# The last two chunks of the second down projection, its norm and the index queries by halves of the tokens

## The reference

```python
x = x + g2 * conv_ffn(h, ffn_w_up[i], ffn_conv_w[i], ffn_conv_b[i], ffn_w_down[i])   # end of layer 0
...
h = rms_norm(x, norm_mix[i]) * (1.0 + sc1) + sh1                                      # start of layer 1
...
proj = h @ w_in
q, lat, qi, ki, wi = jnp.split(proj, [o1, o2, o3, o4], axis=-1)
```

## Time and profile before

| | |
|---|---|
| median of 3 runs | 1906.05 us (1905.83 to 1906.07) |
| the profiled execution's own time | 1905.76 us |
| its span | 1904.0 us |
| busy: PE, PEld | 1877.8 us, 1529.4 us |
| busy: DVE, ACT, POOL | 1081.6 us, 522.3 us, 1189.4 us |

### The profile page before, as it was taken

One profiled execution on the slowest core, in us unless ns is written; L12 is line 12 of the kernel. 1 busy time (PEld: TensorE's weight loads), 2 busy tenths in 40 slices (PEclk: granted clock), 3 DMA queues, 4 the chain that ended last, 5 costly groups with the idle time before them and its releaser, 6 DMA issues.

```text
span 1904.0 us, 26991 instructions
## 1 busy us (share of the span) xinstructions
PE 1877.8 (99%) x9462; PEld 1529.4 (80%) x9462; DVE 1081.6 (57%) x1690; ACT 522.3 (27%) x1085; POOL 1189.4 (62%) x684
## 2 busy tenths in 40 slices
PE   9999899999999999999999999999999999999999
PEld 7867778888888877779888888877766798888887
DVE  5966589998786515654533442144988463433322
ACT  4135300000115424442212121133357331112110
POOL 7641798887665564345766666655757357666673
PEclk9999999999999999999999999989999999999999
DMA  7530277776552231115333333312211123233331
GB/s 280 194 108 3 88 262 240 258 253 220 195 172 78 86 111 56 56 46 176 99 99 99 93 94 99 98 62 85 89 34 34 45 67 116 94 99 99 90 97 66
DMA packets 62325, 221.03 MB, mean 116 GB/s; under 512 B 6907, under 2 KB 7163, under 8 KB 62124
## 3 DMA queue, kind: packets, MB, share of 16 engines
q1 hardware_dynamic: 45216, 161.58, 26.9%
q10 hardware_dynamic: 17036, 58.46, 8.5%
HBM read 217.87 MB, written 2.14 MB: 116 GB/s over the span
## 4 chain that ended last, share of the span: by engine, by line
PE 93%; DVE 3%; POOL 2%; issue 1%; ACT 1%; DMA 0%; SPq 0%; DVEq 0%; POOLq 0%; ACTq 0%
PE bank L332 25%; PE bank L334 25%; PE bank L333 25%; PE bank L974 2%; PE bank L995 1%; PE bank L986 1%; PE bank L367 1%; PE bank L368 1%; PE bank L1102 1%; PE bank L372 1%; PE bank L1154 1%; PE bank L1145 1%; PE bank L463 1%; PE bank L467 1%; PE bank L464 1%
## 5 line engine op out<-in xcount | busy, mean ns | idle before, releaser
L1616 POOL TENSOR_TENSOR w_lo<-raw,w_hi 128x1024 fp32r<-128x1024 f32 x298 | 762.4, 2558 | 24.8
L332 PE MATMUL bank<-a_hi,w_hi 128*128 128x512 f32 (+1 forms) x2000 | 760.3, 380 | 2.1 <-DVE tmp L2417 1.5
L334 PE MATMUL bank<-a_hi,w_lo 128*128 128x512 f32 (+1 forms) x2000 | 758.7, 379 | 0.0
L333 PE MATMUL bank<-a_lo,w_hi 128*128 128x512 f32 (+1 forms) x2000 | 758.6, 379 | 0.0
L1614 POOL TENSOR_SCALAR w_hi<-raw 128x1024 fp32r<-128x1024 f32 x298 | 341.7, 1147 | 597.4 <-PE bank L334 451.6
L332 PEld LDWEIGHTS bank<-a_hi,w_hi 128*128 128x128 f32 x2000 | 376.7, 188 | 74.0 <-DVE tmp L2417 2.0
L333 PEld LDWEIGHTS bank<-a_lo,w_hi 128*128 128x128 f32 x2000 | 376.7, 188 | 70.3
L334 PEld LDWEIGHTS bank<-a_hi,w_lo 128*128 128x128 f32 x2000 | 376.5, 188 | 70.5
L2161 DVE CUSTOM_DVE_ANT_0 y<-y,cond 128x1024 f32<-128x1024 f32 x84 | 209.9, 2532 | 0.0
L2176 DVE SCALAR_TENSOR_TENSOR tmp<-bank,vecs,tmp 128x511 f32<-128x511 f32 x88 | 65.9, 749 | 240.9 <-ACT tmp L1884 240.8
L1884 ACT ACTIVATE tmp<-bank,vecs 128x512 f32<-128x512 f32 x88 | 68.1, 779 | 351.1 <-PE bank L334 347.2
(11 more groups left out here) (314 smaller groups left out, 2113.2 us busy)
## 6 DMA issues: line engine op xcount, KB each, us to landing
raw<-in_stream SPq DMA_DIRECT2D x299, 512.0 KB, 3.5
y<-in_ada ACTq DMA_DIRECT2D x96, 512.0 KB, 4.6
x<-in_x SPq DMA_DIRECT2D x4, 512.0 KB, 6.8
bias<-in_bias ACTq DMA_DIRECT2D x1, 2048.0 KB, 13.5
y<-rel_rows ACTq DMA_DIRECT2D x1, 2048.0 KB, 8.2
bias<-rel_rows ACTq DMA_DIRECT2D x1, 2048.0 KB, 13.2
out<-x SPq DMA_DIRECT2D x8, 256.0 KB, 2.0
cond<-in_c ACTq DMA_DIRECT2D x1, 512.0 KB, 6.9
```

Of the source, the lines that this page charges most:

```text
L332: pe.matmul(o, lhs_hi, rhs_hi, start=start, stop=False, **kw)
L333: pe.matmul(o, lhs_hi, rhs_lo, start=False, stop=False, **kw)
L334: return pe.matmul(o, lhs_lo, rhs_hi, start=False, stop=stop, **kw)
L1616: pool.tensor_tensor(w_lo[:, s, :], raw[:, j, :], f32(w_hi[:, s, :]), ALU.subtract).then_inc(split_ready, 1)
```

## The change

The last two chunks of the second down projection are computed by halves of the tokens, in all eight banks: first half 0 of all tiles, then half 1, both in the order 5, 7, 4, 6, 0, 1, 2, 3. VectorE updates x by half tiles as they come (16 pieces; bank c is read in half 0 before TensorE goes on in its half 1). The norm "mix1" is made in two halves like the others, but with its running sum of squares in `square_sum`, since no bank is free. Its sums of half 0 are put behind the fourth tile of half 1, its spread behind the seventh. The qi tiles run by `pe_early_halves`. POOL makes no low parts of this norm any more; VectorE makes all of them. The first steps of `dve_halved_norm` that scale, take lows and take the inverse are moved to `dve_half_steps` unchanged. The numbering of semaphore counts is changed to fit and left out here.

```diff
-POOL_LOWS = {"battn": (1, 3, 5), "mix1": (1, 3, 5, 7)}
+POOL_LOWS = {"battn": (1, 3, 5)}
...
-HALVED = ("mix0", "ffn0", "ffn1")
+HALVED = ("mix0", "ffn0", "mix1", "ffn1")
...
+DOWN_ORDER = (5, 7, 4, 6, 0, 1, 2, 3)
+DOWN_PIECES = 2 * DC
...
+        def pe_down_halves(pe, name, last, norm):
+            for h in range(2):
+                for n, c in enumerate(DOWN_ORDER):
+                    if h:
+                        pe.wait_ge(x_ready, X_AT[name] + n + 1)
+                    for i in last:
+                        s, j = (START[name] + i) % SPLIT, i % 4
+                        m = pe_three_passes(pe, bank[c][:, tokens_of(h)], w_hi[:, s, c * P:(c + 1) * P], w_lo[:, s, c * P:(c + 1) * P],
+                                            a_hi[:, j, tokens_of(h)], a_lo[:, j, tokens_of(h)], False, i == FC - 1, skip_group_check=True)
+                        if h and n == DC - 1:
+                            m.then_inc(block_done, 1)
...
+                    if h and n == 3:
+                        pe.wait_ge(x_ready, X_AT[name] + DC + 1)
+                        pe_sum_half(pe, norm, 0)
+                    if h and n == 6:
+                        pe_spread_half(pe, norm, 0)
...
+        def act_down_norm(a, update, name, shift):
+            _, high = act_halves(a, update, name, shift)
+
+            def square(p):
+                c, cols = down_piece(p)
+                a.wait_ge(x_ready, X_AT[update] + p + 1)
+                if p % DC == 0:
+                    a.wait_ge(group_used, GROUP_AT[name] - 1)
+                    dst = square_sum[:, GROUP_AT[name] % 2, cols]
+                else:
+                    a.wait_ge(sq_added, down_added(name, p) - 1)
+                    dst = squares[:, down_added(name, p) % 2, cols]
+                a.activation(dst, x[:, c, cols], ACT.Square).then_inc(sq_ready, 1)
+
+            a.preload_act_table(ACT.Sqrt)
+            for p in range(DC + 2):
+                square(p)
+            act_rms(a, name, 0, half_columns(0))
+            for p in range(DC + 2, DC + 5):
+                square(p)
+            for c in range(3):
+                high(0, c)
+                square(DC + 5 + c)
+            for c in range(3, DC):
+                high(0, c)
...
-            pool_lows("mix1")
...
-            pe_down(pe, "down2", 1, norm="mix1")
-
-            pe_norm(pe, "mix1", 1)
-            pe_tiles(pe, "qi", "mix1")
+            pe_down(pe, "down2", 1, halved="mix1")
+            pe_early_halves(pe, "qi", "mix1", "down2", (DC + 6, DOWN_PIECES))
...
+        def dve_down_norm(v, update, name, layer, which, gain, shift):
+            group = square_sum[:, GROUP_AT[name] % 2, :]
...
+            def add(p):
+                added, cols = down_added(name, p), down_piece(p)[1]
+                v.wait_ge(sq_ready, SQUARE_AT[name] + p + 1)
+                v.wait_ge(sq_added, added)
+                v.tensor_tensor(group[:, cols], group[:, cols], squares[:, added % 2, cols], ALU.add).then_inc(sq_added, 1)
+
+            inverse, scale, low = dve_half_steps(v, name, gain, shift)
+            for p in range(DC):
+                residual(p)
+                if p > 1:
+                    add(p - 1)
+            residual(DC)
+            add(DC - 1)
+            residual(DC + 1)
+            residual(DC + 2)
+            inverse(0)
+            residual(DC + 3)
+            add(DC + 1)
+            add(DC + 2)
+            v.wait_ge(rstd_ready, NORM_INDEX[name] + 1)
+            for c in range(DC):
+                scale(0, c)
+                if c < 4:
+                    residual(DC + 4 + c)
+                if c:
+                    low(0, c - 1)
+                if 0 < c < 6:
+                    add(DC + 2 + c)
```

More of the change, by code:

```diff
@@ L601, in sum_columns @@
                 return rstd_bank[:, HALF:HALF + TT]
-            return (bank[0] if name in ("post_ffn", "mix1") else bank[4])[:, 0:TT]
+            return (bank[0] if name == "post_ffn" else bank[4])[:, 0:TT]
         def pe_sum_group(pe, name, g):
@@ L630, in pe_norm, with pe_down @@
             pe_spread(pe, name)
-        def pe_down(pe, name, n, norm=None):
+        def pe_down_halves(pe, name, last, norm):
[9 more added lines that the diff above has]
+                            m.then_inc(block_done, 1)
+                    if not h:
+                        m.then_inc(half_done, 1)
+                    elif n < DC - 1:
+                        m.then_inc(down_done, 1)
+                    if h and n == 3:
[3 more added lines that the diff above has]
+                        pe_spread_half(pe, norm, 0)
+        def pe_down(pe, name, n, norm=None, halved=None):
             def chunk(j, i, start=False):
@@ L657, in pe_down @@
                 pe.wait_ge(lo_ready, LOW_AT[name] + 1 + i)
+            if halved:
+                pe_down_halves(pe, name, last, halved)
+                return
             for c in range(DC):
@@ L1385, in act_halved_norm, with down_piece, down_added @@
             for c in range(5, DC):
+                high(0, c)
+            act_rms(a, name, 1, half_columns(1))
+            for c in range(DC):
+                high(1, c)
+        def down_piece(p):
+            return DOWN_ORDER[p % DC], tokens_of(p // DC)
+        def down_added(name, p):
+            return ADDED_AT[name] + p - 1 - (p > DC)
+        def act_down_norm(a, update, name, shift):
[20 more added lines that the diff above has]
+            for c in range(3, DC):
                 high(0, c)
@@ L2218, in dve_residual_halves, with dve_half_steps @@
             return whole_tile, late_tiles
[L2220 to L2233, removed]
+        def dve_half_steps(v, name, gain, shift):
             def inverse(h):
@@ L2251, in low, with dve_halved_norm, add_piece @@
                                        ALU.subtract).then_inc(lo_ready, 1)
+            return inverse, scale, low
+        def dve_halved_norm(v, name, gain, shift, whole_tile, late_tiles):
+            group = square_sum[:, GROUP_AT[name] % 2, :]
+            def add_piece(p):
+                added, cols = ADDED_AT[name] + p - 1, piece(p)[1]
+                v.wait_ge(sq_ready, SQUARE_AT[name] + p + 1)
+                v.wait_ge(sq_added, added)
+                if p in (7, HALF_PIECES - 1):
+                    v.wait_ge(group_used, GROUP_AT[name] - 1)
+                    dst = group[:, cols]
+                else:
+                    dst = half_sum[:, cols]
+                v.tensor_tensor(dst, half_sum[:, cols], squares[:, added % 2, cols], ALU.add).then_inc(sq_added, 1)
+            inverse, scale, low = dve_half_steps(v, name, gain, shift)
             for c in range(4):
@@ L2276, in dve_halved_norm, with residual @@
                     add_piece(5 + c)
+            low(0, DC - 1)
+            inverse(1)
+            v.wait_ge(rstd_ready, NORM_INDEX[name] + 2)
+            for c in range(DC):
+                scale(1, c)
+                if c:
+                    low(1, c - 1)
+            low(1, DC - 1)
+        def dve_down_norm(v, update, name, layer, which, gain, shift):
+            group = square_sum[:, GROUP_AT[name] % 2, :]
+            def residual(p):
+                c, cols = down_piece(p)
+                if p < DC:
+                    v.wait_ge(half_done, HALF_AT[update] + p + 1)
+                else:
+                    wait_down(v, 1, p - DC)
+                v.scalar_tensor_tensor(x[:, c, cols], bank[c][:, cols], mod(layer, which, c), x[:, c, cols], ALU.mult,
+                                       ALU.add).then_inc(x_ready, 1)
+            def add(p):
+                added, cols = down_added(name, p), down_piece(p)[1]
+                v.wait_ge(sq_ready, SQUARE_AT[name] + p + 1)
+                v.wait_ge(sq_added, added)
+                v.tensor_tensor(group[:, cols], group[:, cols], squares[:, added % 2, cols], ALU.add).then_inc(sq_added, 1)
+            inverse, scale, low = dve_half_steps(v, name, gain, shift)
+            for p in range(DC):
[11 more added lines that the diff above has]
+            v.wait_ge(rstd_ready, NORM_INDEX[name] + 1)
+            for c in range(DC):
+                scale(0, c)
+                if c < 4:
+                    residual(DC + 4 + c)
+                if c:
+                    low(0, c - 1)
+                if 0 < c < 6:
+                    add(DC + 2 + c)
             low(0, DC - 1)
```

36 lines of the change are left out of this document (14 added, 22 removed).

## The result

| | before | changed |
|---|---|---|
| median of 20 runs each | 1905.93 us (1904.90 to 1906.84) | 1908.39 us (1906.78 to 1909.69) |
| the profiled execution's own time, its span | 1905.76, 1904.0 us | 1908.83, 1907.0 us |

The ratio of the times is 1.0014, with a 95% interval of 1.0008 to 1.0020. The change costs about 2.5 us, 0.13%. That is inside the band of 0.2% that the prediction calls no change. The interval leaves 1.0 out, so a small slowdown is shown.

The account below looks back on a forecast made before the run. TensorE, busy 99% of the span, was taken as the bound, with 10.2 us to win around the second down projection's norm. Halves without hold-up -1.7, held additions +3.7 (+1.9 together), clock +1.0: +2.9 on 1906.05, 1909.0 us (1904.0 to 1911.1).

Parts of the forecast that it names:

- Half products: TensorE's 256-column products in down chunks and qi: 0.120 us each, 1.92 us more in all.
- The second half of the down tiles: Last two down chunks, half 1: norm of half 0 hidden, no tile waits, last down tile ends at 1253.39.
- The loop without a hold-up: First two qi tiles: low, addition, square, high take 1.77 us per chunk; alone, 1.7 us faster than before.
- The held additions: VectorE's SBUF additions 11 and 12 wait for POOL's low splits: 3.7 us in the loop, making it 1.9 us slower.
- The clock: TensorE, starved in the first qi tiles, falls to level 0.50 until about 1268.0: 1.0 us more.
- The second rival: First qi tiles: the low clock lasts about 10 us, until 1272.2; 4.9 us slower, 1910.9 us; chance 0.18.
- POOL and the weights: POOL's weight splits: qi's third block hidden, done by 1260.7; ki's block ready with a margin of some 0.5 us.
- The first: Rival: additions aren't held or slip in ahead of POOL; 1.7 us faster, 1904.3 us with none held; chance 0.22.
- The third: Rival: the feed of the first qi tiles keeps up with TensorE; 7.1 us faster, 1898.9 us; chance 0.09.
- The first term: Down chunks to first ki product: halving without held additions or clock loss makes it 1.7 us faster.

Follow-up runs that it names:

- e1: The changed kernel, but the running sum of squares of half 1 in PSUM bank 7 instead of square_sum; 1903.61 us, ratio 0.9991 to the kernel before.
- e3: The changed kernel plus 12, 36, 36 and 12 unread 128-column TensorE products ahead of chunks 0 to 3 of the first qi pair; 1908.07 us, ratio 1.0013.
- e8: The kernel before, with all mix1 low parts on VectorE, none on POOL, and no second ScalarE pass over odd chunks; 1904.98 us, ratio 0.9998.
- e5: The changed kernel, but squares 13 to 15 have their own buffers in tmp; additions stay in SBUF and in place; 1908.31 us, ratio 1.0013.
- e7: e4 with updates 11 to 13 made during the spread, additions 9 to 15 after half 0's last low, half 1's sums and spread later; 1902.02 us, ratio 0.9982.
- e4: The changed kernel with highs before late squares, squares 13 to 15 in tmp, additions 11 to 15 after half 0's last low, half 1's sums later; 1903.18 us.
- e2: The changed kernel, but POOL waits for addition 13 before splitting the third qi block; additions stay in SBUF; 1907.43 us, ratio 1.0008.

## Why the prediction was right

It gave 1909.0 us (1904.0 to 1911.1) with 0.65 on no change, and 1908.39 was measured. Step by step:

- **Half products.** 0.120 us, as the earlier trace rows had it. The formula for isolated products of the Trainium skill (TensorE: Matmul & The Clock Gate, Back-to-back issue gap) gives 109 ns, an estimate; the trace disagrees again (1241.16, 1241.28, 1241.40 and so on).
- **The second half of the down tiles.** The forecast had the first scale at 1252.94 and the last down tile's end at 1253.39. The scale came at 1252.94 and the last product was issued at 1253.34, so it ended at 1253.46. From the first product to the end of the last it took 12.30 us instead of 12.09: the changes between sums, spread and products were sized 0.2 too small. No down tile waited for VectorE.
- **The loop without a hold-up.** 1.77 us forecast, 1.73 in e1. Without the held additions the seam was to be 1.7 us shorter than before; e1 measured 1.5, and the 0.2 of the step above are the difference.
- **The held additions.** Forecast: the addition issued at 1255.16 ends at 1257.2, the one issued at 1258.57 at 1261.0, together 3.7 us (its own ends give 1.6 + 2.0 = 3.6). The trace: 1255.07 to 1257.23 and 1258.54 to 1260.86, and the seam of e3 less that of e1 gives 3.69. This was the step that decided the sign. The row at 512 columns carried over to 256. So did the rule of the Trainium skill (SBUF — State Buffer, Who interferes with whom), and here too the trace agrees: 2.16 and 2.32 us with two SBUF inputs beside a POOL split, 0.42 with the sum in PSUM beside the same split. The lows write to SBUF as well but read one of their tiles from PSUM, and the one from 1254.67 took 0.48 beside the split of 1254.59; so writing to SBUF isn't what holds an addition.
- **The clock.** Forecast 1.0 us with a return at about 1268.0. The low level lasted from about 1257.9 to 1268.1, and its price was 0.93 (e3). The first pair's half 0 ended with the sums at 1269.21, where the forecast had 1268.2 + 1.0. The forecast took 6 us of the low level behind the restart of steady work, and the trace has 6.3 (from 1261.79). The second rival, 10 us behind the restart, did not come. That the 6 us fitted is partly luck: in e8 TensorE restarts at 1260.22 and the level is back at 1264.9, only 4.7 us later. What the kernel before, the changed one, e5 and e8 have in common is that the low level lasts 10.2 us from its fall, and the forecast gave no time for the fall.
- **POOL and the weights.** The qi splits were done at 1260.6, before their use. ki's high split started at 1283.05 and its low split ended at 1286.57, 0.56 before its use: the margin of some 0.5 held.

**The rivals.** The first (additions free, 1.7 us faster) did not happen by itself and was made by e1. It counted on small errors of start times, and the starts were right to 0.1 us. The third (the feed keeps up, 7.1 us faster) fell by the same loop: even e7, which has no additions in it, comes 3.2 short.

**The size.** The terms were -1.7, +3.7 and +1.0, and came as -1.5, +3.69 and +0.93: the seam grew by 3.12, where the forecast had 2.9. The first term was the one mis-sized, by 0.2. The medians grew by 2.46 only. The trace is one execution of 1908.83 us, 0.4 above its kernel's median, while that of before lay 0.2 below its own. The difference between forecast and median, 0.6 us, is of the size of this spread, and nothing in the steps has to explain it.

## What to carry to other kernels

A step that is cut off an engine frees that engine for its next work, and this work may meet somebody else's: ask of each engine that the change makes idle what it will start, and which operand memories that touches. An addition of two SBUF operands inside a loop of VectorE was held until a POOL instruction of 2.4 us ended, at 512 columns and at 256; put the sum in PSUM, or move the additions out of the loop that feeds TensorE. What halving a norm is worth depends on what else stands in VectorE's list in the first chunks: the same halves made the seam 3.1 us longer, 1.5 shorter (e1) or 3.9 shorter (e7), by the place and order of seven additions and two updates.

## What the runs showed of the hardware that I had not expected

- The hold-up goes both ways. POOL's high split that began under a held addition took 1.22 us (1256.92, until 1258.14) against 1.04 for the same split in e1. The second low split thus starts later, and meets the next addition earlier in its life. In e8 a high split that began at 1252.01, under an addition that ran from 1251.83 to 1252.51, took 1.41.
- The held additions ended 0.28 to 0.30 us behind POOL's instruction, nearly the 0.33 that such an addition takes of VectorE: it seems to start only when POOL ends. This is read from the ends; no row shows the start.
- Additions that wait for each other and follow directly start 0.53 us apart (five in 2.55 us in e7, three in 1.49 in e4, the last of each taking 0.42), against 0.33 to the next start when another instruction follows (1262.17 to 1262.50 in the changed kernel). Moved together they are dearer, and this was not wholly hidden: in e4 TensorE waited 0.44 us for them before the sums of half 1, and in e7 the sums started at 1265.27, just behind the last addition's end (1265.21) and some 0.2 us late, which is more than the 0.1 by which e7 missed its expectation.
- The low clock lasted 10.2 us in the kernel before, in the changed one, in e5 and in e8, but 6.8 us in e2. In the changed kernel it came in the second of TensorE's waits, which were 1.2 and 2.4 us long; in e2 it came after waits of 1.2, three of about 0.7, 0.2 and 1.55; and in e1, with a wait of 1.2 and three of about 0.7, it did not come. What lies between wasn't tried.
